# An mLSTM recurrence rearranged: the next unit's scores and keys placed between a unit's numerators and increments

## The reference

```
s   = (q k^T) * w_intra                         # scores, weighed
num = a_inter * (q C) + s v                     # numerators
den = a_inter * (q n) + sum(s)
h   = num / max(|den|, exp(-m))                 # norm
C   = decay * C + (k * g)^T v                   # increments, state update
n   = decay * n + sum(g * k)
```

## Time and profile before

| | us |
|---|---|
| median of 3 runs | 3647.92 (3646.84, 3647.92, 3660.62) |
| profiled execution | 3665.19, its span 3663.4 |
| PE busy in the span | 3246.3 |
| DVE busy | 1449.2 |
| ACT busy | 832.5 |
| POOL busy | 256.4 |

### The profile page before, as it was taken

The page is one execution under the profiler, slowest core; times in us unless marked ns, Lnnn a source line. Parts: engine busy times, 40 slices in busy tenths (PEclk is TensorE's granted clock), DMA queues, the critical chain, the costliest instruction groups (busy, mean ns, idle before and its releaser), DMA issues. The chain is left out here.

```text
span 3663.4 us, 48224 instructions
## 1 busy us (share of the span) xinstructions
PE 3246.3 (89%) x17267; PEld 1766.4 (48%) x17268; DVE 1449.2 (40%) x4224; ACT 832.5 (23%) x1602; POOL 256.4 (7%) x321
## 2 busy tenths in 40 slices
PE   6999966799999599999997899899999779898983
PEld 3666624744455343444443455477775434343431
DVE  2343263555564411111111688666656421111114
ACT  1111122365521000000001344355551100000000
POOL 0000003400050000000000000000002000000001
PEclk8999967899999699999998999899999889999997
DMA  9600086300042369999784322100003158898998
GB/s 348 253 23 29 12 340 199 94 1 1 1 139 82 145 267 381 358 354 376 284 313 187 105 75 83 69 1 1 1 1 135 51 218 321 311 375 338 404 397 319
DMA packets 283213, 676.96 MB, mean 185 GB/s; under 512 B 24004, under 2 KB 36468, under 8 KB 282996
## 3 DMA queue, kind: packets, MB, share of 16 engines
q1 hardware_dynamic: 252596, 560.12, 40.6%
q0 software_dynamic: 20176, 76.55, 5.7%
q10 hardware_dynamic: 10224, 37.23, 2.5%
HBM read 579.32 MB, written 94.50 MB: 184 GB/s over the span
## 5 line engine op out<-in xcount | busy, mean ns | idle before, releaser
L2567 PE MATMUL ex_ps_g<-w_ring,ex_xT 128*64 128x512 f32 x1696 | 406.7, 635 | 71.9 <-issue 71.9
L2598 PE MATMUL ps_y<-w_ring,ex_hT 128*64 128x512 f32 x1696 | 399.0, 602 | 0.0
L2579 PE MATMUL ps_u<-w_ring,ex_xT 128*64 128x256 f32 x3392 | 387.2, 381 | 1.0 <-DMA w_ring<-in_w 1.0
L2579 PEld LDWEIGHTS ps_u<-w_ring,ex_xT 128*64 128x64 f32 x3392 | 242.8, 137 | 143.5 <-issue 38.8
L2567 PEld LDWEIGHTS ex_ps_g<-w_ring,ex_xT 128*64 128x64 f32 x1696 | 130.0, 146 | 319.6 <-issue 319.0
L1654 PE MATMUL of_ps_r<-of_w,cat 128*128 128x512 f32 (+1 forms) x608 | 258.1, 581 | 3.0 <-ACT cat L1737 3.0
L408 PE MATMUL ps_r<-w,hT 128*128 128x512 f32 (+1 forms) x640 | 249.9, 547 | 2.9 <-issue 2.9
L2663 DVE SCALAR_TENSOR_TENSOR ex_hr<-ex_th,ex_ps_g 128x512 f32<-128x512 f32 x53 | 36.4, 688 | 469.2 <-ACT ex_th L2641 469.2
L2598 PEld LDWEIGHTS ps_y<-w_ring,ex_hT 128*64 128x64 f32 x1696 | 107.6, 136 | 178.0 <-issue 178.0
L1381 PE MATMUL mo_ps_o<-mo_w,mo_cT 128*128 128x512 f32 x416 | 185.8, 598 | 1.4 <-DMA mo_w<-in_e_w_out 0.9
L2108 DVE TENSOR_SCALAR_CACHE_REDUCE oa_sx<-oa_ps_s 128x512 f32<-128x512 f32 (+1 forms) x288 | 160.2, 598 | 58.4 <-PE oa_ps_s L2024 57.3
(11 more groups left out here) (483 smaller groups left out, 4361.8 us busy)
## 6 DMA issues: line engine op xcount, KB each, us to landing
w_ring<-in_w SPq DMA_DIRECT2D x768, 512.0 KB, 10.5
ml_staging<-in_w_ada SPq DMA_DIRECT2D x14, 2048.0 KB
y_dram<-zeros POOLq DMA_DIRECT2D x2, 14080.0 KB, 65.4
y_dram<-ex_y ACTq DMA_DIRECT2D x53, 512.0 KB, 6.3
ml_spare<-in_w_ada SPq DMA_DIRECT2D x6, 2048.0 KB, 12.7
ml_arena<-ml_rows SPq DMA_DIRECT2D x40, 256.0 KB, 4.2
f_dram<-mo_f SPq DMA_DIRECT2D x18, 512.0 KB, 2.8
w<-in_e_w_in SPq DMA_DIRECT2D x2, 4096.0 KB, 25.3
```

The source lines that it names most:

```text
L2567: mm = pe.matmul(ps_g[rows, :], xT[:, k, rows], weight(k // 2)[:, h, (k % 2) * DE:(k % 2 + 1) * DE], start=k == 0, stop=k == KD - 1)
L2579: mm = pe.matmul(ps_u[rows, f, 0:256], xT[:, k, rows], weight(4 + k // 2)[:, h, at:at + 256], start=k == 0, stop=k == KD - 1)
L2598: mm = pe.matmul(ps_y[rows, half, :], hT[:, k, rows], weight(8 + k)[:, h, half * 512:(half + 1) * 512], start=k == 0, stop=k == 3)
```

## The change

PE goes by units and not by pairs. The scores and keys of unit 0 stand ahead of the body; then, for each unit u: scores of u+1, numerators of u, keys of u+1, increments of u. Scores and keys of both directions now use bank 0 of `ps_s` and `ps_k`; the second banks of these two hold the numerators of direction 1 (three heads in `ps_s`, one in `ps_k`), and `ps_n` those of direction 0. Numerators of u wait for the norm and the update of u-2 (the start value of h_out is one higher, and c_out >= u+3), and the increments of u for the update of u-1 (c_out >= u+4). ACT does exponentials and scaled keys unit by unit. DVE weighs u+1 ahead of norm and update of u, with unit 0 weighed ahead of the body. On PE and DVE the last body, which has no next unit behind its last one, is written out straight, and the loop has three turns in place of four. SP and POOL are as before.

```diff
+        def sums(d, h):
+            if d == 0:
+                return place(ps_n, h)
+            return ps_s[:, 1, h * 129:(h + 1) * 129] if h < 3 else ps_k[:, 1, 0:129]
...
+        def turns_to_last(eng, body):
+            body(0, 0, lambda par: (par, 1 - par))
+            with eng.Fori(0, NTL // 2 - 1) as i:
+                body(i + 1, i * 2 + 2, lambda par: (i * 2 + 2 + par, i * (-2) + 9 - par))
+            body(NTL // 2, NTL, lambda par: (NTL + par, NTC + 1 - par))
...
+                def scores(u, b):
+                    pe.wait_ge(staged, u * 5 + 25)
+                    pe.wait_ge(sw_ready, u + 2)
+                    for h in range(BH):
+                        mm = pe.matmul(ps_s[:, 0, h * P:(h + 1) * P], ks[:, b, h, :], qs[:, b, h, :], start=True, stop=True)
+                    mm.then_inc(s_done, 1)
+
+                def keys(u, b):
+                    pe.wait_ge(kg_ready, u + 2)
+                    for h in range(BH):
+                        mm = pe.transpose(ps_k[:, 0, h * P:(h + 1) * P], ks[:, b, h, :], g.ident)
+                    mm.then_inc(k_done, 1)
+
                 def body(it, step, tiles):
...
+                    for b in range(4):
+                        d, u = b % 2, it * 4 + b
+                        more = b < 3 or not isinstance(it, int) or it < NTL // 2
+                        if more:
+                            scores(u + 1, (b + 1) % 4)
+
+                        pe.wait_ge(sw_ready, u + 3)
+                        pe.wait_ge(h_out, u + 1)
+                        pe.wait_ge(c_out, u + 3)
+                        for h in range(BH):
+                            pe.matmul(sums(d, h), sw[:, d, h, :], vv[:, b, h, 0:129], start=True, stop=False)
+                            mm = pe.matmul(sums(d, h), qa[:, b, h, :], C[:, d, h, 0:129], start=False, stop=True)
+                        mm.then_inc(n_done, 1)
+                        if more:
+                            keys(u + 1, (b + 1) % 4)
+
+                        pe.wait_ge(kg_ready, u + 3)
+                        pe.wait_ge(c_out, u + 4)
+                        for h in range(BH):
+                            mm = pe.matmul(place(ps_c, h), kg[:, d, h, :], vv[:, b, h, 0:129], start=True, stop=True)
+                        mm.then_inc(c_done, 1)
+
+                scores(0, 0)
+                keys(0, 0)
+                turns_to_last(pe, body)
...
-                dve.sem_inc(h_out, 1)
+                dve.sem_inc(h_out, 2)
                 dve.sem_inc(c_out, 4)
+
+                def weigh(u, d):
+                    dve.wait_ge(s_done, u + 1)
+                    dve.wait_ge(w_ready, u + 5)
+                    dve.wait_ge(n_done, u + 1)
+                    dve.tensor_tensor(sw[:, d, :, :], ps_s[:, 0, :].rearrange("p (h t) -> p h t", t=P), wt[:, d, :, :], ALU.mult).then_inc(sw_ready, 1)
...
+                    for b in range(4):
+                        d, u = b % 2, it * 4 + b
+                        tile = tiles(b // 2)[d]
+                        if b < 3 or not isinstance(it, int) or it < NTL // 2:
+                            weigh(u + 1, 1 - d)
```

More of the change, by code:

```diff
@@ L749, in _ @@
                 pe.sem_inc(c_done, 4)
-                def body(it, step, tiles):
[L752 to L780, removed]
@@ L782, in _ @@
-                turns(pe, body)
+                def scores(u, b):
[9 more added lines that the diff above has]
+                    mm.then_inc(k_done, 1)
@@ L815, in body @@
                 def body(it, step, tiles):
[L816 to L834, removed]
+                    for b in range(4):
+                        d, u = b % 2, it * 4 + b
+                        act.wait_ge(staged, u * 5 + 25)
+                        act.wait_ge(sw_ready, u + 1)
+                        for h in range(BH):
+                            w = act.activation(wt[:, d, h, :], tm[:, b, h, :], ACT.Exp, bias=cur[:, b, 0, h:h + 1])
+                        w.then_inc(w_ready, 1)
+                        act.wait_ge(k_done, u + 1)
+                        act.wait_ge(c_done, u + 3)
+                        for h in range(BH):
+                            w = act.activation(kg[:, d, h, :], ps_k[:, 0, h * P:(h + 1) * P], ACT.Copy, scale=cur[:, b, 1, h:h + 1])
+                        w.then_inc(kg_ready, 1)
                 turns(act, body)
@@ L954, in body @@
                         c.turn(it - 1, 4 * 5)
[L955 to L987, removed]
@@ new lines, in body @@
+                    for b in range(4):
+                        d, u = b % 2, it * 4 + b
+                        tile = tiles(b // 2)[d]
+                        if b < 3 or not isinstance(it, int) or it < NTL // 2:
+                            weigh(u + 1, 1 - d)
+                        dve.wait_ge(n_done, u + 3)
+                        three, fourth = (ps_n[:, 0, 0:387], ps_n[:, 1, 128:129]) if d == 0 else (ps_s[:, 1, 0:387], ps_k[:, 1, 128:129])
+                        dve.tensor_copy(dn[:, 0, 0:3], three.rearrange("p (h e) -> p h e", e=129)[:, :, 128]).then_inc(*c.up())
+                        dve.tensor_copy(dn[:, 0, 3:4], fourth).then_inc(*c.up())
+                        own()
+                        dve.scalar_tensor_tensor(out=dn[:, 1, :], in0=dn[:, 0, :], scalar=-1.0, in1=dn[:, 0, :], op0=ALU.mult, op1=ALU.max).then_inc(*c.up())
+                        own()
+                        dve.tensor_tensor(dn[:, 2, :], dn[:, 1, :], cur[:, b, 2, :], ALU.max).then_inc(*c.up())
+                        own()
+                        dve.reciprocal(dn[:, 1, :], dn[:, 2, :]).then_inc(*c.up())
+                        own()
+                        for h in range(BH):
+                            o = L.hb[:, bass.ds(tile, 1), h * P:(h + 1) * P]
+                            w = dve.scalar_tensor_tensor(out=o, in0=sums(d, h)[:, 0:P].unsqueeze(1), scalar=dn[:, 1, h:h + 1], in1=o, op0=ALU.mult, op1=ALU.add)
+                        w.then_inc(h_out, 1)
+                        dve.wait_ge(c_done, u + 5)
+                        for h in range(BH):
+                            w = dve.scalar_tensor_tensor(out=C[:, d, h, 0:129], in0=C[:, d, h, 0:129], scalar=cur[:, b, 3, h:h + 1],
+                                                         in1=place(ps_c, h), op0=ALU.mult, op1=ALU.add)
+                        w.then_inc(c_out, 1)
@@ L988, in body @@
                     if not isinstance(it, int):
-                        c.turned(NTL // 2)
-                turns(dve, body)
+                        c.turned(NTL // 2 - 1)
+                weigh(0, 0)
+                turns_to_last(dve, body)
 def even_attend(nc, g, A, L):
```

## The result

The changed kernel takes 3604.53 us, median of four runs (3597.47 to 3608.12), against 3647.38 (3644.51 to 3660.62) of the kernel before: the ratio is 0.9867 [0.9838, 0.9897], and a second set of runs gives 0.9875 [0.9856, 0.9894]. By the ratios that is 48 and 46 us less than 3648, by the medians 43 in both sets (3647.38 - 3604.53, 3653.11 - 3610.15). Forecast were 29, with at most 46: the direction was right and the gain about one and a half times the forecast one.

The account below looks back on a forecast made before the run. A chain of waits bounds the recurrence, afterwards the load loop: e(3) at 618.4, 15 units at 4.83 to 690.9, a last unit of 5.1, end 696.0 for 724.67. So 3647.9 - 28.7 = 3619 us, range 3602 to 3640.

Parts of the forecast that it names:

- The ten stalls of 2.36 us go: Recurrence: PE's numerators, idle once per pair until DVE's state update, would need only the update of u-2.
- the wait ahead of the increments that the prediction had as covered: Recurrence, PE: increments of u wait for update u-1, claimed to be over by then, with 1.9 us of slack.
- The load loop: Recurrence: load issue to POOL's start 6.25, staging, PE's work, back to issue; 14.5 us for three units, 4.83 per unit.
- Stage end 696.0, -28.7 us: End of the mLSTM recurrence, claimed at 696.0 us in place of 724.67, a gain of 28.7 us.
- e(3): Moment at which the increments of unit 3 end on PE, claimed at 618.4 us.
- The head: Recurrence's first units: POOL's staging stays, DVE is the chain, with small operations 5.9 us too long in all.
- e(0): Moment at which the increments of unit 0 end on PE, claimed to stay at 602.96 us.
- the first pass over straight code: Head of the recurrence: claimed reason why seven small DVE operations took 0.52 to 1.87 us in place of 0.16.
- The clock: PE's granted clock: full from the head on, as new gaps are 0.8 us; attention still starts at 0.50.
- the gain would have been 23: Recurrence, opposing case: clock drops remain with short gaps; five at 1.2 us make 6 us.
- Nothing later in the kernel was started during this stage, so the later stages only move.: Stages after the recurrence: claimed to keep their length, so the stage's 28.7 us carry over to the median.
- what its own first pass costs, 0 to 6 us: Last body written out on PE and DVE: cold code costs 0 to 5.9 us; 0 taken, 6 kept for the range.

Follow-up runs that it names:

- e_banks: Kernel before with the change's banks, waits and ACT order, but PE and DVE still going by pairs: 3639.01 us, 0.9954.
- e_long: Changed kernel with two more broadcasts of the same size added to each unit's load: 3642.79 us, one run.
- e_split: Changed kernel with each load's two broadcasts issued before the wait for increments; only the values wait, on their own semaphore: 3583.81 us, 0.9811.
- e_single: Changed kernel with DVE's small norm operations rewritten so that none has two SBUF inputs: 3601.96 us, 0.9854.
- e_peeled: Kernel before with only the recurrence's last body written out straight on PE and DVE: 3630.32 us, 0.9938.
- pad_pe_64: Kernel before with 64 no-ops ahead of all of PE's work: 3617.3 us, 0.9908.
- after_pad: Changed kernel with 209 no-ops ahead of PE's work: 3633.66 us, 0.9952.

## Why the prediction was right in the stage and wrong in the sum

- *The ten stalls of 2.36 us go.* Right: neither of PE's waits of the earlier trace rows is left in the first trace. In the second, the wait ahead of the increments that the prediction had as covered shows once, 2.56 us, behind the DVE operation of 3.66 us. e_banks shows what that hangs on: the order, not the banks.
- *The load loop is the new bound, 4.83 us per unit.* Right, measured (687.64 - 614.57) / 15 = 4.87, and 5.00 in the second trace; issue to start 6.31 for 6.25. e_long and e_split move the unit both ways as the loop says, and with it open the unit is PE's 4.0 to 4.1.
- *Stage end 696.0, -28.7 us.* It ended at 692.50 and 698.89; the gain is 31.2 and 20.8 by the two pairs of traces, 26 on the mean. The stage before differs by 6.5 us between its own traces (to e(3) 9.4 the one way, with more low clock and nine long operations on DVE for five, behind it 3.5 the other), which is more than the step was off.
- *The head.* e(0) came at 600.16 for 602.96, and e(0) to e(3) took 14.4 for 15.4 us; in the second trace 602.62 and 16.4. Its reason, "the first pass over straight code", was wrong: the long rows are DVE behind POOL. L972 of the earlier trace rows ends at 602.36 + 1.87 = 604.23, and POOL's L709 of the same moment at 602.96 + 1.26 = 604.22: the two stood in one trace, and I did not lay them side by side. The Trainium skill, page GPSIMD Engine Reference, section 1. Specifications, has the reason: GpSimd and VectorE share an interface to SBUF, and a VectorE instruction with both inputs in SBUF contends for it. e_single agrees, 24 long rows to none.
- *The clock.* Right for the first trace: 1.00, the 2.4 GHz level, from 600 to 690 us, where the earlier trace rows had 0.86 over every second pair. In the second it is 0.96, with two drops where the prediction had none. Attention starts at 0.52, near the 1.2 GHz level, in the first trace of either kernel, and at 0.72 in the second of either. By the rule that the prediction cites from the Trainium skill, page TensorE: Matmul & The Clock Gate, section A second HAM failure mode: psum-queue depth-cycling, the gain would have been 23. The traces bear it out in part: no drop after the gaps of 0.3 to 2.1 us of the first trace, and one after 2.56 and one after 2.20 us in the second.
- *"Nothing later in the kernel was started during this stage, so the later stages only move."* **This step failed.** The premise stands; the conclusion doesn't. The experts became 25 us shorter, about half of the gain, with no line of theirs changed. The runs put in its place: the second copy of PE's last body shifts PE's later code by 303 instructions, and a loop of PE that stalls for 45.7 us in the expert rounds of layer 1 stalls for 30.5, one in layer 0 for 19.9 in place of 26.2. I had priced the copy by what its own first pass costs, 0 to 6 us, and not by what it does to the code behind it. e_peeled has that gain without the recurrence's, pad_pe_64 without any change of work, after_pad loses most of it.

That the stalls are the fetch of code is inferred, from "issue" as releaser, the instruction packets of 16 KB in each of the 190 stalls, their end behind the last packet and the return at 256; no packet names its engine. The Trainium skill, page Advanced Engine Details and Errata, section ISA Cache, gives a line of 16 KB as 256 instructions, with which the return at 256 agrees. Rounds of 3.4, 8.6 and 14.5 us hold one, two and three packets, some 6 us from start to start; why a round at one place needs three and at another none is open, and so is why layer 0 doesn't come back in full (721.7 and 718.7 for 725.4).

## What to carry to other kernels

When a change writes code out once more or takes some out, an engine's later loops move too: compare the length of stages that the diff doesn't touch, and pad the engine's program by 64, 128 and 192 no-ops before a gain or loss of 1% is put down to the idea. When a stall behind a shared buffer goes, follow the next unit's inputs back to what allows their load: here the loop over load, staging and increments was the new bound, 4.87 and 5.00 us per unit where it gave 4.83. Splitting a load by what each part really waits for was worth another 0.6% (0.9811 for 0.9867 to 0.9875); some 5 us of that are the experts', whose code it moved too.

## What the runs showed of the hardware

- PE's loops have places that cost: 64 no-ops made the kernel 33 us faster, 256 brought layer 1 back to 867.7 of 868.2 us; a second copy of a body in DVE's code did nothing (869.4). The stalls hold one, two or three instruction packets of 16 KB each: 3.1 to 4.6, 5.3 to 9.4 and 14.4 to 14.9 us.
- A VectorE operation on four elements with two inputs in SBUF takes 0.16 us, or until a GpSimd operation of 128x512 beside it ends, mostly up to 1.3 us and once 3.66 us over four of them; with one input in PSUM (e_single) none took over 0.3.
- Two more broadcasts beside three transfers lengthened the load from 6.3 to 11.0 us, at a DMA share of 0.78.
